# Hybrid GLA + SSD + MoE block in float32: split weights of the first three token pairs kept in DRAM later

## The reference

```
h    = rmsnorm(x);  proj = h @ w_in
q, k, v, g, a_low, z, xbc, dt_raw = split(proj)
gla  = gated linear attention(q, k, v, log_sigmoid(a_low @ w_alpha_up + b))   # chunks of 64, 4 heads
ssd  = Mamba-2 scan(silu(conv4(xbc)), softplus(dt_raw), A, D)                 # 8 heads, 2 groups
x    = x + [groupnorm(gla) * silu(g), groupnorm(ssd * silu(z))] @ w_out
h2   = rmsnorm(x);  top-4-of-32 experts, clamped SwiGLU of width 1024;  x = x + moe(h2)
out  = rmsnorm(x)
```

## Time and profile before

| | |
|---|---|
| median of three runs | 3492.0 us |
| the profiled execution's own time | 3497.87 us |
| its span | 3496.3 us |
| TensorE busy (PE), weight loads (PEld) | 98%, 91% |
| VectorE (DVE), ScalarE (ACT), GpSimd (POOL) | 61%, 47%, 18% |
| chain that ended last | PE 94%, DMA 2%, DVE 1%, ACT 1%, issue 1% |
| DMA | 817.12 MB, 234 GB/s on average |
| stores of split units | 16 of 2 MB, 12.4 us to landing |
| loads of split units | 112 of 2 MB, 9.0 us to landing |
| raw loads of `w_in` | 12 of 1 MB, 10.7 us to landing |

### The profile page before, as it was taken

How to read it: one execution, slowest core, us unless ns; L and a number is a source line. 1 busy time by engine, 2 the same in 40 slices (tenths; PEclk the granted TensorE clock), 3 DMA queues, 4 the chain that set the end, 5 groups by cost and what they waited for, 6 DMA issues and landing times.

```text
span 3496.3 us, 59353 instructions
## 1 busy us (share of the span) xinstructions
PE 3427.6 (98%) x22487; PEld 3172.3 (91%) x22487; DVE 2140.2 (61%) x2762; ACT 1652.5 (47%) x2155; POOL 625.9 (18%) x848
## 2 busy tenths in 40 slices
PE   7999999999998999999999999999999999999997
PEld 6888888888888999999999999988888899999996
DVE  4555355445455555556566666667766777777777
ACT  4443333333233444444444444455555565665665
POOL 1011111111113111111111121122211221221213
PEclk9999999999999999999999999999999999999998
DMA  9888887887865555666666566566665767767778
GB/s 374 332 315 323 303 294 283 301 302 277 299 252 187 173 168 169 183 182 184 180 191 193 184 202 201 176 211 213 200 216 187 222 219 222 221 212 235 229 241 295
DMA packets 470677, 817.12 MB, mean 234 GB/s; under 512 B 19533, under 2 KB 416989, under 8 KB 454176
## 3 DMA queue, kind: packets, MB, share of 16 engines
q1 hardware_dynamic: 438752, 712.33, 59.1%
q0 software_dynamic: 24320, 75.95, 9.3%
q10 hardware_dynamic: 7488, 27.27, 2.2%
HBM read 716.65 MB, written 98.96 MB: 233 GB/s over the span
## 4 chain that ended last, share of the span: by engine, by line
PE 94%; DMA 2%; DVE 1%; ACT 1%; issue 1%; POOL 0%; SPq 0%; another core or an unknown queue 0%; POOLq 0%; ACTq 0%; DVEq 0%
PE acc L2400 22%; PE pp L1980 14%; PE acc L2402 11%; PE acc L2396 10%; PE acc L2397 10%; PE acc L2398 10%; PE pp L1970 5%; PE tpm L2376 2%; PE tpm L2370 2%; PE tp L1949 2%; DMA uraw<-in_w_in 1%; PE seg L2025 1%; PE seg L2081 1%; PE pm L2100 1%; PE pm L2009 1%
## 5 line engine op out<-in xcount | busy, mean ns | idle before, releaser
L1821 DVE TENSOR_TENSOR wlo<-raw,whi 128x2048 fp32r<-128x2048 f32 x384 | 878.9, 2289 | 303.4 <-ACT whi L1248 303.4
L2400 PE MATMUL acc<-xhl,whi 128*128 128x512 f32 (+3 forms) x2304 | 768.2, 386 | 0.0
L1248 ACT ACTIVATE whi<-raw 128x2048 fp32r<-128x2048 f32 x384 | 733.9, 1911 | 21.8 <-DMA raw<-in_moe_w_gate 20.8
L662 POOL TENSOR_TENSOR gate_op<-gate_op 1x1 f32<-1x1 f32 x351 | 162.7, 464 | 2762.6 <-ACT ybuf L1263 838.8
L2402 PE MATMUL acc<-xhl,wlo 128*128 128x256 f32 (+3 forms) x2304 | 624.4, 271 | 0.0
L2396 PE MATMUL acc<-xhl,whi 128*128 128x272 f32 (+3 forms) x1792 | 534.9, 298 | 1.5 <-DVE xhl L1833 1.5
L2397 PE MATMUL acc<-xhl,whi 128*128 128x272 f32 (+3 forms) x1792 | 530.2, 296 | 0.0
L2398 PE MATMUL acc<-xhl,wlo 128*128 128x272 f32 (+3 forms) x1792 | 530.1, 296 | 0.0
L2400 PEld LDWEIGHTS acc<-xhl,whi 128*128 128x128 f32 x2304 | 432.0, 188 | 66.7
L2402 PEld LDWEIGHTS acc<-xhl,wlo 128*128 128x128 f32 x2304 | 437.3, 190 | 0.0
L2400 PE MATMUL acc<-ahl,whi 128*128 128x512 f32 (+3 forms) x1152 | 387.6, 388 | 0.7 <-DVE ahl L1862 0.7
(11 more groups left out here) (328 smaller groups left out, 5821.8 us busy)
## 6 DMA issues: line engine op xcount, KB each, us to landing
u<-split_d SPq DMA_DIRECT2D x112, 2048.0 KB, 9.0
raw<-in_moe_w_gate SPq DMA_DIRECT2D x128, 1024.0 KB
raw<-in_moe_w_up SPq DMA_DIRECT2D x128, 1024.0 KB
raw<-in_moe_w_down SPq DMA_DIRECT2D x128, 1024.0 KB
split_d<-u SPq DMA_DIRECT2D x16, 2048.0 KB, 12.4
uraw<-in_w_in SPq DMA_DIRECT2D x12, 1024.0 KB, 10.7
xin<-in_x ACTq DMA_DIRECT2D x14, 512.0 KB, 9.0
xres<-in_x ACTq DMA_DIRECT2D x14, 512.0 KB, 10.4
```

The source lines that it names most:

```text
L662: pool.tensor_tensor(gate_op[0:1, 0:1], gate_op[0:1, 1:2], gate_op[0:1, 1:2], ALU.add).then_inc(gate_ran, 1)
L1248: act.activation(whi[:, q % RING, :, :], raw[:, q % RING, :, :], ACT.Copy).then_inc(a_hi, 1)
L1821: dve.tensor_tensor(wlo[:, q % RING, :, :], raw[:, q % RING, :, :], whi[:, q % RING, :, :].bitcast(F32), ALU.subtract).then_inc(v_lo, 1)
L2400: pe.matmul(into[:, 0:2 * n].rearrange("p (c n) -> p c n", c=2), hi_, of[:, k, :, 0:n], start=(k == 0), stop=False)
```

## The change

Splitting is spread over three pairs. Pair 0 splits units 0 to 11 and stores none. Pair 1 loads all 16 units raw, splits them and stores units 0 to 3 and 12 to 15. Pair 2 loads units 0 to 3 and 12 to 15 split, units 4 to 11 raw, splits these and stores them. From pair 3 on nothing changes. Units 0 to 2 of pair 1 are loaded raw at the end of pair 0, and units 0 to 3 of pair 1 are split there. The number of stores stays 16, the number of splits goes from 16 to 36. Waits, counters and the places of the splits in the programs of ScalarE and VectorE change with it.

```diff
         def stored(eng, n):
-            eng.wait_ge(d_st[n % 4], 16 * (n // 4 + 1))
+            eng.wait_ge(d_st[n % 4], 16 * (1, 3, 4, 2)[n // 4])
+        def split_at(s, n):
+            return s == 0 and n < 12 or s == 1 or s == 2 and 4 <= n < 12
+        def splits(s, n):
+            return (n, 12 + n, 24 + n)[s] + 1
...
             def raw_unit(s, n, at):
                 if n >= 4:
                     released(sp, s, n - 4, at)
-                    stored(sp, n - 4)
+                    if s == 1 and n < 8 or s == 2 and n >= 8:
+                        stored(sp, n - 4)
+                elif s == 1:
+                    released(sp, 0, n + 8, 0)
...
             def body(s, at):                      # SP
                 if at == 0:
+                    for n in range(4, 12):
+                        raw_unit(0, n, 0)
                     for n in range(3):
-                        store_unit(n)
-                    raw_unit(0, 4, 0)
-                    store_unit(3)
-                    raw_unit(0, 5, 0)
-                    for n in range(6, 12):
-                        raw_unit(0, n, 0)
-                        store_unit(n - 2)
-                    store_unit(10)
+                        raw_unit(1, n, 1)
                 elif at == 1:
-                    for n in range(3, 12):
-                        unit(1, n, 1)
-                    raw_unit(1, 12, 1)
-                    for n in range(13, 16):
+                    raw_unit(1, 3, 1)
+                    store_unit(1, 0)
+                    store_unit(1, 1)
+                    raw_unit(1, 4, 1)
+                    store_unit(1, 2)
+                    raw_unit(1, 5, 1)
+                    store_unit(1, 3)
+                    for n in range(6, 14):
                         raw_unit(1, n, 1)
-                        store_unit(n - 1)
+                    for n in range(14, 16):
+                        store_unit(1, n - 2)
+                        raw_unit(1, n, 1)
+                    store_unit(1, 14)
+                    unit(2, 0, 2)
+                    store_unit(1, 15)
+                    unit(2, 1, 2)
+                    unit(2, 2, 2)
+                elif at == 2:
+                    unit(2, 3, 2)
+                    for n in range(4, 12):
+                        raw_unit(2, n, 2)
+                        if n >= 6:
+                            store_unit(2, n - 2)
+                    for n in range(12, 16):
+                        unit(2, n, 2)
+                        if n < 14:
+                            store_unit(2, n - 2)
...
# ScalarE's body (all with the pair as first argument now)
-                split = at == 0
+                split = at < 3
                 if split:
-                    unit_hi(6)
-                    unit_hi(7)
+                    unit_hi(s, 6)
+                if at == 0:
+                    unit_hi(s, 7)
...
                     gla_squares(b)
+                    if split:
+                        unit_hi(s, 7)
...
-                if post:
-                    gates(q * 2 + 1)
                 if more:
                     norm_xn(a + 4)
                 if split:
-                    unit_hi(11)
+                    unit_hi(s, 11)
+                if post:
+                    gates(q * 2 + 1)
...
-                if at == 1:
-                    unit_hi(12)           # and 13, 14, 15 at three later places
+                if at < 2:
+                    unit_hi(*((1, 0), (1, 12))[at])
...
# VectorE's body
                 if rec:
                     qkv(b, 1, p)
                     gla_decay(b)
                     gla_add(b)
+                    if split:
+                        unit_lo(s, 4)
                 dt_zb(s)
-                if split:
-                    unit_lo(6)
-                    unit_lo(7)
+                if at == 0:
+                    unit_lo(s, 6)
+                    unit_lo(s, 7)
+                elif split:
+                    unit_lo(s, 5)
                 if rec:
                     masked(b)
+                    if split:
+                        unit_lo(s, 6)
...
                     mixed_lo(a - 2, 0)
+                    if split:
+                        unit_lo(s, 7)
                     ssd_in(b, 1)
...
                 dt_la(s)
-                if split:
-                    unit_lo(9)
                 if rec:
                     ssd_y(b, 1, p)
                     ssd_decay(b)
+                if split:
+                    unit_lo(s, 9)
                 if post:
                     h2_T(q * 2 + 1, a - 2)
...
-                if at == 1:
-                    unit_lo(12)           # and 13, 14, 15 at three later places
+                if at < 2:
+                    unit_lo(*((1, 0), (1, 12))[at])
...
             def ready(s, n, at):                  # TensorE
-                if at == 0 or at == 1 and n >= 12:
-                    pe.wait_ge(v_ul, n + 1)
+                if split_at(at, n):
+                    pe.wait_ge(v_ul, splits(at, n))
```

83 lines of the change are left out of this document (40 added, 43 removed).

## The result

The changed kernel takes 3506.26 us in the median of six runs (3503.86 to 3507.65), the kernel before 3491.92 us (3483.57 to 3493.67, six runs): a ratio of 1.0043, with a 95% interval of 1.003 to 1.0056. It is slower by about 14 us, which is over the 0.2% that can be told. The forecast was 3498 us, with a range of 3485 to 3509 us. The time lies in the range, but at its far side, 8 us above the forecast and on the number of rival (2).

The account below looks back on a forecast made before the run. TensorE, busy 98% of the span, was taken as the bound. Terms -13.2 + 1.9 + 1.3 + 6.0 (second pair) + 7.4 (third pair) + 2.7 (clock) = +6.1 us on 3492.0 gave 3498 us, range 3485 to 3509.

Parts of the forecast that it names:

- rival (2): Waits of 2.8 us also cost the clock: three more prices of 2.7 us, giving 3506 us; chance 0.25.
- -13.2: First pair: us saved as two TensorE waits shrink and half clock behind them goes, with stores gone from the queue.
- +1.9: End of first pair: new wait in us before the scores, from VectorE's added low part of unit 0 and state sum.
- +1.3: Border to second pair: us more before its first product, as unit 2's low part stands ahead of `hlo`.
- first wait: First pair, TensorE's 3.77 us wait for a normalised input tile, hanging on unit 3's raw load: claimed to stay.
- the ring order: Each DMA engine takes a queue's descriptors in order, so a store behind a load does not slow it.
- rival (3): Transfers share instead of queueing: first wait goes (-4.8 us), unit 3 late (up to +3.4), stores crowd (+3); 3500 us; chance 0.1.
- 2.8 us before the SSD products: Second pair: TensorE waits 2.8 us for SSD inputs, delayed by unit 7's low part on VectorE.
- 2.7 us before the turned q and k: Second pair: 2.7 us more TensorE wait on `mT`, since nothing on VectorE absorbs units 10 and 11.
- 0.5 us at the scores: Second pair: last part of its 6.0 us, from a wait of 1.2 us where 0.6 stand now.
- h2 turn: Third pair: TensorE's transposes wait 4.55 us for it, behind unit 9's parts; the largest new wait.
- Rival (1): Cover holds: new VectorE and ScalarE work fits beside TensorE in the second and third pair; 3482 us; chance 0.17.

Follow-up runs that it names:

- e3: Changed kernel with 25 matmuls of 128 columns added ahead of the SSD products in both the second and third pair; 3522.08 us.
- e12: Changed kernel with 25 matmuls of 128 columns added ahead of the SSD products in the third pair only; 3508.02 us.
- e4: Changed kernel with unit 4's high part behind the decay exponentials (third pair) and unit 11's low part behind the mT turn (second and third); 3500.55 us.
- e10: e8 with low parts of units 9 and 15 moved behind bank-freeing adds and unit 14's raw load ahead of unit 12's store; 3484.16 us.
- e11: Changed kernel with all sixteen stores in the second pair, third pair as before the change, low parts re-placed, units 9 and 15 behind bank-freeing adds; 3484.09 us.
- e1: Changed kernel with unit 7's high part directly behind unit 6's in all three pairs; 3507.78 us.
- e8: Changed kernel with same loads, splits and stores, several low parts moved later in VectorE's program, plus e4's two moves; 3501.59 us.
- e6: Changed kernel with all sixteen units stored in the second pair; third pair still splits units 4 to 11 but stores nothing; 3507.01 us.

## Why the prediction was right on its range and wrong in its sum

**First pair: right.** Foretold -13.2, +1.9 and +1.3, together 10.0 us earlier; it was 11.95. The waits of 4.56 and 4.03 us became 0.96 us and nothing, the stretches behind at 1.00. The scores wait 0.97 us (1.9 foretold), `hlo` adds 1.25 (2.09 for 0.84; 1.3 foretold). The 1.95 us beyond the forecast are the 0.9 us at the scores and about 1 us behind the first wait, where the clock stood at 0.68 instead of 0.50.

**First wait: right.** It is 3.12 us (3.77 before). Unit 3 came in at 26.95 us, as the earlier trace rows have it with 26.92, with no store left in the queue. Only 0.03 us moved, so the store behind this load did not slow it; the ring order that the prediction used stands, and rival (3) falls. Transfers ahead of a load do: raw loads took a median of 5.1 us in the quiet first pair (50 to 105 us), where 6 were assumed, and 6.6 to 14.6 us behind a 2 MB transfer in the two pairs that follow (median 5.9 over all 36 of after, 10.3 in the earlier trace rows).

**Second pair: the size right by luck, two of three places wrong.** Foretold 6.0 us, it is 7.66: 3.7 us more idle and 3.9 us more busy, where all was to be idle. The 2.8 us before the SSD products came as 2.81. The 2.7 us before the turned q and k did not come. VectorE's chain was right (`mT` done at 203.8 us, 203.1 by the forecast, moved to the real start of the pair), but TensorE came there at 205.3 us and not at 200.5: it had lost 3.3 us at half clock and waited 1.00 us before the decays. The 0.5 us at the scores did not come either. Two terms that failed and two that were missing made up for each other.

**The clock behind 2.8 us: the step that failed first.** "For the waits of 2.8 us no row lies near; I take no loss, with 2.7 each as the other end." The granted clock was 0.50 for 6.0 us behind the first and 0.58 over 6.4 us behind the second, about 3 us each. Rival (2), at 0.25, had the mechanism. That it has the time too, 3506 us, is luck: it priced three such waits at 2.7 us each and two came; by its terms the second pair loses 11.4 us and the third 12.8, and they lost 7.66 and 17.6. What the half clock alone is worth in the end is open: the one trial of it, e3, filled the waits with matmuls that took as much as they saved.

**Third pair: the step that failed most.** Foretold 7.4 and 2.7 for the clock, 10.1 us; it is 17.6. The h2 turn, the largest term, came as 1.09 us instead of 4.55, in part for the same reason as in the second pair (in e3 and e12, at full clock, it is 2.6 us). In its place stand 4.64 us before the turned q and k of one tile, behind `mT`, and 1.91 before those of the other, neither of which is in the sum; "After it VectorE is ahead again" did not hold. The sentence that failed is "Each store is queued behind the next raw load and has a unit and a half of products [...]; I cost this at nothing, with up to 3 us". It asked when the store's buffer is needed. It should have asked what the next raw load stands behind, and what is queued on ScalarE and VectorE behind the split that waits for it. e4 took the two waits away without touching a transfer and got 5.7 of the 14 us back.

**What the loss is.** VectorE and the DMA engines can do all that the change adds (e10, e11). The changed kernel loses because splits stand ahead of what TensorE needs at once, though it needs them only later (the products of unit 7 start at 183.1 us, 13 us behind the SSD products that its low part had held up), while VectorE is idle for over 7 us some steps further. Rival (1), cover enough, was right on the amount and wrong on the order. The single steps interlock: moving one (e1) gave nothing in the median, two (e4) 5.7 us, all with a slip in two (e8) 4.7 us, which its ratio's interval does not tell from the changed kernel's, all with the slips mended (e10) 22 us. How much of e10's gain each move brings, and how much the two swapped transfers, was not tried.

## What to carry to other kernels

When work is added to an engine that is busy for two thirds of a stretch, walk its program in order and ask of each added instruction who waits for the one behind it; put it in the engine's own idle time, past everything that the bounding engine wants first, and count banks and buffers as well as values. In a DMA queue ask of each load what is issued ahead of it: 1 MB loads of 5 us took 7 to 15 us behind a 2 MB transfer, and a store behind the load cost nothing. If a moved step has a store that waits for it, the loads behind that store have moved too. And before the waits of one profile are weighed against another's, look at two profiles of the same stretch of program: here they differed by up to 5 us in 130.

## What the runs showed of the hardware

Waits of 2.81 us were enough to bring TensorE's clock from 2.4 to 1.2 GHz for about 6 us, at 170.1 and at 305.6 us, and in e8 one of 3.48 us at 185.5 us. Yet a wait's length alone does not tell what it costs. One of 2.61 us in e12 (321.9 us) was followed by a clock of 1.00, one of 2.60 us in e6 (280.5 us) by 0.72 over 6 us. Each changed kernel here has a wait of 1.66 us between 113 and 121 us, before the last SSD products of the first pair. In four of them it ends between 113.8 and 115.3 us: the clock from 115 to 120 us was 1.00 in the changed kernel, 0.66 in e11, 0.63 in e10 and 0.50 in e8.

In the changed kernel the half clock behind a wait of 2.81 us cost 3.3 us: 18.8 us from the SSD products to the decays, waits left out, for 15.5 us in e3. A stretch filled with 25 matmuls of 128 columns (5.6 us) kept the clock up and cost as much as it saved.

50 more matmuls ahead of a loop, not 25, made TensorE load its instructions anew in the passes of the loop: 94 packets for 75, and pauses of 2 to 3.4 us that the profile puts down to issue.
